# A second attention in four query tiles a head, with one shared tile for the last 16 queries of eight heads

## The reference, cut to what matters

```python
q = jnp.concatenate([q[..., :QK_NOPE_DIM], apply_rope(q[..., QK_NOPE_DIM:], cos, sin)], axis=-1)
k = jnp.concatenate([k_nope, jnp.broadcast_to(k_rope, (B, L, N_HEADS, QK_ROPE_DIM))], axis=-1)
for start in range(0, L, Q_BLOCK):
    s = jnp.einsum('bqhd,bkhd->bhqk', qb, kb).astype(jnp.float32) * scale
    s = jnp.where(mask[None, None], s, -jnp.inf)          # causal
    p = jax.nn.softmax(s, axis=-1).astype(vb.dtype)
    outs.append(jnp.einsum('bhqk,bkhd->bqhd', p, vb))
```

## Time and profile before

| | |
|---|---|
| median of 3 runs | 2306.0 us (2302.53 to 2307.81) |
| the profiled execution, its time and its span | 2310.08 us, 2308.3 us |
| granted TensorE clock, mean | 0.949 |
| PE busy, DVE busy, ACT busy, POOL busy | 89%, 42%, 43%, 38% |
| the second attention, first scores to the first product behind it | 1165.98 to 1337.28 us |

### The profile page before, as it was taken

The page is one execution under the profiler, slowest core; times in us unless marked ns, Lnnn a source line. Parts: engine busy times, 40 slices in busy tenths (PEclk is TensorE's granted clock), DMA queues, the critical chain, the costliest instruction groups (busy, mean ns, idle before and its releaser), DMA issues.

```text
span 2308.3 us, 35210 instructions
## 1 busy us (share of the span) xinstructions
PE 2043.1 (89%) x12788; PEld 1798.7 (78%) x12792; DVE 980.6 (42%) x1683; ACT 981.7 (43%) x1606; POOL 888.2 (38%) x498
## 2 busy tenths in 40 slices
PE   3699789998899999977878898999999669999997
PEld 2587577875677778756767787999999559999997
DVE  5862782115433422246667726242400674333202
ACT  2212663323555552243356625454522445555422
POOL 1244322432234344412643325434344554343443
PEclk8799998999999999987989999999999789999998
DMA  8372002321122233201200012323232003222232
GB/s 302 115 243 88 6 15 88 94 82 64 46 91 92 90 103 107 91 28 55 80 12 0 0 37 65 100 82 94 88 101 92 28 19 92 91 89 93 91 101 73
DMA packets 55370, 186.27 MB, mean 81 GB/s; under 512 B 6912, under 2 KB 10240, under 8 KB 55296
## 3 DMA queue, kind: packets, MB, share of 16 engines
q1 hardware_dynamic: 53920, 183.66, 24.6%
q10 hardware_dynamic: 1376, 1.59, 0.2%
HBM read 183.13 MB, written 2.10 MB: 80 GB/s over the span
## 4 chain that ended last, share of the span: by engine, by line
PE 76%; DVE 13%; issue 5%; ACT 3%; POOL 2%; DMA 1%; DVEq 0%; ACTq 0%; SPq 0%; POOLq 0%
PE PS L553 63%; PE PS L822 2%; PE PS L767 2%; PE PS L612 1%; PE PS L723 1%; PE PS L679 1%; DVE small L1967 1%; PE PS L600 1%; DVE ada_acc L1821 1%; DVE pool_s L298 1%; PE PS L740 1%; POOL X L1186 1%; DMA ada_w<-ada 1%; DVE small L1918 1%; DVE work L2080 1%
## 5 line engine op out<-in xcount | busy, mean ns | idle before, releaser
L1092 POOL TENSOR_TENSOR w_lo<-w_raw,w_hi 128x1024 fp32r<-128x1024 f32 x289 | 699.9, 2428 | 1131.8 <-ACT w_hi L1264 1130.6
L553 PE MATMUL PS<-H_hi,w_lo 128*128 128x264 f32 (+1 forms) x2152 | 584.7, 324 | 67.8 <-POOL H_lo L1226 25.8
L1264 ACT ACTIVATE w_hi<-w_raw 128x1024 fp32r<-128x1024 f32 x293 | 309.0, 1058 | 782.7 <-PE PS L553 717.2
L553 PE MATMUL PS<-H_lo,w_hi 128*128 128x264 f32 (+1 forms) x2152 | 576.0, 320 | 0.0
L553 PE MATMUL PS<-H_hi,w_hi 128*128 128x264 f32 (+1 forms) x2152 | 576.0, 320 | 0.0
L553 PEld LDWEIGHTS PS<-H_hi,w_lo 128*128 128x128 f32 x2152 | 365.7, 192 | 114.3 <-issue 45.1
L553 PEld LDWEIGHTS PS<-H_lo,w_hi 128*128 128x128 f32 x2152 | 367.5, 192 | 27.3
L553 PEld LDWEIGHTS PS<-H_hi,w_hi 128*128 128x128 f32 x2152 | 365.7, 192 | 28.1
L2080 DVE SCALAR_TENSOR_TENSOR work<-PS,vec,work 128x526 f32<-128x526 f32 (+3 forms) x264 | 188.3, 755 | 465.1 <-ACT work L1560 455.3
L553 PE MATMUL PS<-mid_hi,w_lo 128*128 128x264 f32 (+1 forms) x880 | 223.8, 308 | 3.6 <-DVE work L2080 3.6
L553 PE MATMUL PS<-mid_hi,w_hi 128*128 128x264 f32 (+1 forms) x880 | 223.1, 307 | 0.0
(11 more groups left out here) (257 smaller groups left out, 3048.1 us busy)
## 6 DMA issues: line engine op xcount, KB each, us to landing
w_raw<-stream SPq DMA_DIRECT2D x293, 512.0 KB, 3.5
ada_w<-ada SPq DMA_DIRECT2D x48, 512.0 KB, 5.9
X<-xT SPq DMA_DIRECT2D x1, 2048.0 KB, 9.6
yT<-X SPq DMA_DIRECT2D x8, 132.0 KB, 1.7
rel_raw<-rel ACTq DMA_DIRECT2D x4, 256.0 KB, 2.6
yT<-X SPq DMA_DIRECT2D x8, 124.0 KB, 1.7
vec<-vecs SPq DMA_DIRECT2D x1, 390.0 KB, 2.9
cos_t<-rope ACTq DMA_DIRECT2D x1, 264.0 KB, 2.8
```

Source lines behind the costliest of these rows:

```text
L553: last = pe.matmul(out[:, c0 + a:c0 + b], w, x[:, a:b], start=start and i == 0, stop=stop and i == 2)
L1092: gp.tensor_tensor(w_lo[:, o], w_raw[:, o], w_hi[:, o].bitcast(F32), ALU.subtract)\
L1264: return act_.activation(out, in_, ACT.Copy, scale=scale)
```

## The change

The second attention is written anew after the manner of the first one.

- **Units.** A head has four full tiles of 128 queries. The two heads of a pair take turns, tile by tile. The last 16 queries of eight heads (four pairs) stand below each other as one tile of 128 rows. With two such tails there are 66 units (`UNITS2`) instead of 80. A tail unit stands in the fourth and in the eighth pair, between the second and the third query tile.
- **Scores of the tail.** They build up over four pairs in a PSUM bank of their own (`tail_bank`). Each head puts its 16 queries at its own place in a window of zeros (`zq_hi`, `zq_lo`), so that a product of 128 rows adds only to its own 16. That is six products of 512 columns a pair (`tail_scores`). The scores of the 16 queries against the last 16 keys are six products of 16 columns and a mask, in a corner of the bank of the first tile of the odd head (`own_scores`). ACT copies them to `self_s`.
- **Ahead by two.** `scores` and `maximum` run two units ahead of `turn_over` and `normalize`. There are three score banks and four exponential buffers, and `weights` follows two units behind.
- **Staging.** Key parts hold the rotary rows too and are doubled over pairs. Query parts are rounded by tile (both heads, 256 columns). Values are split for all heads in the `uv` stage (ACT copies, DVE subtracts). The weights of the tail against all values are 60 products of 32 columns a group (`tail_outputs`).
- **Weight stream.** The transposed weights now lie over `w_raw`, so loads behind the first four `wo` blocks wait for the end of this attention.
- One small copy (`sel_tail`) is added to the set-up. The loops over pairs are unrolled.

The core of the diff, PE first:

```diff
+UNITS2 = []
+for _p in range(PAIRS2):
+    for _i in range(NQ1):
+        if _i == 2 and _p in TAIL_P2:
+            UNITS2.append((_p, None, None))
+        UNITS2 += [(_p, _i, 0), (_p, _i, 1)]
...
+                def scores(m):
+                    p, i, par = MAIN2[m]
+                    pe.wait_ge(kl2_ok, 2 * p + par + 1)
+                    pe.wait_ge(ql2_ok, NQ1 * p + i + 1)
...
+                    if m >= 3:
+                        pe.wait_ge(p2_ok, UNIT2[MAIN2[m - 3]] + 1)
...
+                    own = i == 0 and par == 1
+                    if own:
+                        own_scores(p, out)
...
+                def own_scores(p, out):
+                    pe.wait_ge(zl2_ok, p + 1)
+                    for par in range(2):
+                        tail_passes(out[:, own_bank2], p, par, slice(S1, S2), par == 0)
...
+                for u, (p, i, par) in enumerate(UNITS2):
+                    if i is not None and m < len(MAIN2):
...
+                        scores(m)
+                        if MAIN2[m][1:] == (1, 1):
+                            tail_scores(MAIN2[m][0])
+                        m += 1
...
+                    turn_over(u)
+                    if i == 2:
...
+                        outputs(p, par, False)
+                    elif i == 0 and p:
+                        outputs(p - 1, par, True)
+                    if i == 3 and par == 0 and p in TAIL_P2:
+                        tail_outputs(p // GROUP2)
```

POOL, ACT and DVE:

```diff
+                for p in range(1, PAIRS2):
+                    for par in range(2):
+                        lower_k(p, par)
+                    for i in range(NQ1 - 1):
+                        lower_q(p, i)
+                    lower_zq(p)
+                    lower_q(p, NQ1 - 1)
...
+                for u, (p, i, par) in enumerate(UNITS2):
+                    if u >= 2:
+                        weights(u - 2)
+                    exps(u)
+                    nxt = p + 1
+                    if i == 0 and par == 1 and p:
+                        round_q(p, 3)
+                    if nxt < PAIRS2:
+                        if i == 1:
+                            round_k(nxt, par)
+                        if i and par == 1:
+                            round_q(nxt, i - 1)
+                        if i == 3 and par == 1:
+                            round_zq(nxt)
+                    if i == 1 and p:
+                        take_out(p - 1, par)
...
+                for u, (p, i, par) in enumerate(UNITS2):
+                    if u >= 2:
+                        weights(u - 2)
+                    normalize(u)
+                    if u + 2 < len(UNITS2):
+                        maximum(u + 2)
+                    if i == 1 and p:
+                        take_out(p - 1, par)
...
-            for t in (k2_hi, k2_lo, v2_hi, v2_lo):
-                v.memset(t[:, :].bitcast(F32), 0.0).then_inc(zero_ok, 1)
```

More of the change, by code:

```diff
@@ L117 @@
 FOX1 = PAIRS1 // 2
+PAIRS2 = H2 // 2
+GROUP2 = 4
+TAIL_P2 = tuple(range(GROUP2 - 1, PAIRS2, GROUP2))
+UNITS2 = []
[4 more added lines that the diff above has]
+        UNITS2 += [(_p, _i, 0), (_p, _i, 1)]
+UNIT2 = {x: n for n, x in enumerate(UNITS2)}
+MAIN2 = [x for x in UNITS2 if x[1] is not None]
+ZQ = 112 + META + 112
 COL2 = 248
@@ L137 @@
 NVEC = _v
-SET_UP = 14
+SET_UP = 15
 ADA_ORDER = (1, 0, 2, 3, 4, 5)
@@ L704, in attention2 @@
             def attention2():
[L705 to L741, removed]
@@ L773, in step @@
[L773 to L777, removed]
-                    if t % nq == 3:
-                        outputs(p, t // nq, False)
-                    if t == nq + 1:
-                        outputs(p, 0, True)
-                    elif t == 1 and not first:
-                        outputs(p - 1, 1, True)
-                    turn_over(p, t)
@@ L791, in _ @@
+                for par in range(2):
+                    outputs(PAIRS2 - 1, par, True)
             pe.wait_ge(set_up, SET_UP)
@@ L1047, in _ @@
                 last.then_inc(w_used, 1)
-            for k in range(4):
-                pe.wait_ge(free[k], FREE0["wo"][k] + 1)
             attention2()
-            pe.wait_ge(o_lo, 8 + 1)
+            pe.wait_ge(o2_lo, 2 * PAIRS2)
+            pe.wait_ge(ot_lo, 2 * len(TAIL_P2))
             def ox2(k):
@@ L1545, in attention2, with round_q, round_zq @@
-                act_.wait_ge(pv_done, 2)
-                for i in range(ns):
-                    stage_head(0, 0, i)
-                over_pairs(act_, pairs, U, step)
-                weights(pairs - 1, U - 1)
-                take_out(pairs - 1)
+                def round_q(p, i):
+                    if p:
+                        act_.wait_ge(s2_full, 8 * (p - 1) + 2 * i + 2)
+                    copy(q_part2(q2_hi, i), q_raw2(p, i)).then_inc(qh2_ok, 1)
+                def round_zq(p):
+                    if p:
+                        act_.wait_ge(s2_full, 8 * (p - 1) + 5)
+                    copy(zq_part2(zq_hi), zq_raw2(p)).then_inc(zh2_ok, 1)
@@ L1552, in ffn @@
+                for u in range(len(UNITS2) - 2, len(UNITS2)):
+                    weights(u)
+                take_tail(1)
+                for par in range(2):
+                    take_out(PAIRS2 - 1, par)
             def ffn(up, down, T, layer, mid0):
@@ new lines, in normalize @@
+                def normalize(u):
+                    v.wait_ge(p2_ok, u + 1)
+                    c = u % 4
+                    s, q = small[:, 4 + c:5 + c], small[:, 8 + c:9 + c]
+                    if UNITS2[u][1] is None:
+                        chain.done(v.tensor_tensor(s, s, small[:, 12:13], ALU.add))
+                        chain.wait()
+                    chain.done(v.reciprocal(q, s))
+                    chain.wait()
+                    pb = p_buf2(u)
+                    v.tensor_scalar(pb, pb, q, None, ALU.mult).then_inc(pn2_ok, 1)
```

534 lines of the change are left out of this document (326 added, 208 removed).

## The result

The changed kernel takes 2321.4 us (median of five runs, 2320.7 to 2328.4) against 2306.0. The ratio is 1.0078, with a 95% interval of 1.006 to 1.0096. It is 15.4 us slower. The forecast was 2303 with a range of 2288 to 2317.

A forecast was written before the change was run, and what follows sets the result against it. No engine but the loop through PE, DVE and ACT was taken as the bound of the second attention. Its sum, 20.7 + 137.9 + 7.8 + 12.1 = 178.5 us against 181.4, gave 2306.0 - 2.9 = 2303, range 2288 to 2317.

The forecast's parts named there:

- from 0 to 1.45: In a pair, from PE turning over d of head 0 (time 0) until `lower_zq` lets the next a1 scores start.
- a0, b1, c0 and d0: Query tiles a to d of heads 0 and 1; PE was to idle 0.7, 1.3, 1.0, 0.5 us before their transposes.
- 18.7 to 18.8 and 0.3: A pair at full clock: PE's 13.9 us plus 4.9 idling; 0.3 added for DVE products that meet a POOL subtraction.
- The prices of the narrow products: PE products of few columns, in `own_scores` and the tail outputs, were taken at 0.115 us each.
- The rival of decoupled lists: Running ahead by two decouples the lists: a pair costs little over PE's sum, 15.3 us, kernel 2272; chance 0.08.
- the one of narrow products at double cost: Products with 16 rows or columns cost double: `own_scores` 0.5 us more a pair, tails 3 together; 2310; chance 0.07.
- I take 0.7, which is more than today's mean of 0.5: Clock falls were to cost 0.7 us a pair, out of 0 to 2, giving 19.7 us a pair.
- both places: At time 0 and at b1 in each new pair, PE works only about half of 3 us.
- 6.9 us of tail outputs on PE: A group's tail adds 60 products of 32 columns on PE, 6.9 us, counted behind each tail unit.
- the start: From the end of `uv` to d0 of the first pair turned over: 20.7 us, bounds 18 to 24.
- the end: Second group's tail outputs 6.9 us, last transposes and two late outputs 3.5, take-out to `wo` 1.7: together 12.1.
- The clock falls more often: Rival: falls at gaps around `own_scores` and b1 and in two blocks of 60 narrow products; 2315 (2311-2320); chance 0.22.

The follow-up runs named there:

- `zq` early: Changed kernel with `round_zq` moved one tile ahead on ACT and `lower_zq` two ahead on POOL: 2306.2 us.
- the wide block: Changed kernel with the tail outputs as 15 products of 512 columns a block instead of 60 of 32: 2312.1 us.
- The fill run: Changed kernel with dummy 256-column products where PE sits idle, before `own_scores` and the transposes of d0, a0, b1 and c0: 2319.6 us.
- the fixes: Three edits to the changed kernel: `round_zq` and `lower_zq` earlier (2306.2 us alone), tail scores behind c1's scores (2319.0), tail outputs as 512-column products (2312.1).
- all three: Changed kernel with `round_zq` and `lower_zq` earlier, tail scores behind c1's scores in six pairs, and 512-column tail outputs together: 2279.9 us.
- The fill run beside wide blocks: Changed kernel with dummy products in PE's gaps and tail outputs as 512-column products: 2302.4 us.
- the kernel with later tail scores: Changed kernel with `tail_scores` moved from behind b1's scores to behind c1's scores in six pairs: 2319.0 us.

## Why the prediction was wrong

**Right: the loop and its waits.** I forecast that PE would wait for `lower_zq` from 0 to 1.45. The trace has 1.31 us idle before `own_scores` in six of the seven later pairs; in the seventh the tail block hides it. The idle times of 0.7, 1.3, 1.0 and 0.5 us ahead of a0, b1, c0 and d0 are 0.57, 1.60, 0.96 and 0.46. At full clock the changed pair is 17.7 us (`zq` early, no fall) and 1.55 for the wait, or 19.2. My 18.7 to 18.8 and 0.3 make 19.1. The prices of the narrow products at full clock (0.115; measured 0.111) were right too. The rival of decoupled lists fell, and so did the one of narrow products at double cost as such.

**Wrong: the clock, in the pairs.** The step was "I take 0.7, which is more than today's mean of 0.5". The four plain pairs take 20.3, 23.4, 20.2 and 20.5 us from d0 to d0, a mean of 21.1. That is 1.9 above the 19.2, where the forecast has 0.7. Three of the pairs have one fall, which costs 1.0 to 1.3 us, and one has two, which cost 4.2. I had found both places where PE works half of the time, and then priced them by the old kernel, in which only every second pair falls.

**Wrong: the clock, in the narrow blocks.** The step was "6.9 us of tail outputs on PE". The blocks took 10.9 and 10.6, 7.7 us more in all, and left the clock low for what followed. The sum counted falls behind idling only, though the rival named these blocks. A stretch of narrow products with no idle time did the same, and the wide block without them did not.

**Wrong: the start and the end, in part.** The start took 22.9 us instead of 20.7. The first scores already come 6.0 us behind the end of `uv` instead of 4.8. The next fence shows why, from the timelines of POOL and DVE in the changed kernel: DVE's subtraction of 64x528 takes 0.70 us alone and 2.42 us beside POOL's subtraction for a weight block. The other 1.0 us of the start stays open. The end took 17.4 us instead of 12.1: 3.7 of it is the block. Most of the other 1.6 is the low clock behind the block: of the last 24 output products the first twelve take 2.6 us and the others 1.5.

```profile
1152.68 2.35 POOL L1187 TENSOR_TENSOR w_lo<-w_raw,w_hi 128x1024 fp32r<-128x1024 f32 x1 [6.32 <-ACT w_hi L1385]
1153.16 2.42 DVE L2120 TENSOR_TENSOR k_lo<-K,k_hi 64x528 fp32r<-64x528 f32 x1 [0.78 <-ACT k_hi L1385]
...
1156.81 0.70 DVE L2120 TENSOR_TENSOR k_lo<-K,k_hi 64x528 fp32r<-64x528 f32 x1
```

| from the end of `uv` | forecast | measured |
|---|---|---|
| to d0 of the first pair | 20.7 | 22.9 |
| the seven pairs and the first tail block | 145.7 | 156.9, of it 4.0 the block and 7.2 the pairs |
| to the start of `wo` | 12.1 | 17.4, of it 3.7 the block |
| sum | 178.5 | 197.1 |

One slip is of no weight: the forecast gives `uv` 0.7 us more (0.6 measured), but its sum, 20.7 + 137.9 + 7.8 + 12.1, leaves the 0.7 out.

**The rival that held.** "The clock falls more often" named both places and gave 2311 to 2320, with a chance of 0.22. It is what happened. It priced the pairs at 8 us (7.2 measured) and the blocks at 4 (7.7 measured). Start and end had no price in it, so its range ended 1 us too low. The Trainium skill (TensorE: Matmul & The Clock Gate, section "A second HAM failure mode: psum-queue depth-cycling") says that PE idling a little between groups, bank after bank, makes the clock go back and forth. The fill run agrees: with the gaps filled all four plain pairs stay at 1.00, and none of them did before. But I had let the trace of the old kernel outweigh the page, when it was the new kernel's gaps that counted.

**What the clock hides.** A fall costs about 1 us, and filling all gaps gave 1.8 us in 2321. From this one would say that the clock matters little. It mattered 9.7 us once the blocks were wide. At the same time the fixes gain more together (41.5 us) than singly (15.2 + 2.4 + 9.3 = 26.9); by the stages it is 40.4 against 28.7. The mean clock of the stage goes with this: 0.88, 0.81 and 0.87 with one fix, 0.95 with all three. That each fix takes away gaps or narrow stretches by which the others lost is my reading. The fill run beside wide blocks bears it out, and for the tail scores it isn't shown.

## What to carry to other kernels

A small operation behind a large one on two lists, here a 32-column rounding behind exponentials and a 256-column subtraction, can cost its wait once a round and the clock on top. Put it where its data are free, not where its turn comes. Don't price a stretch of PE by its columns alone. 60 products of 32 columns have a quarter of the columns of 15 products of 512, and were slower: 6.7 us at 0.111 us each, and 10.9 as the clock fell, against 3.9. When several stalls sit in one loop, try the fixes together before one of them is written off.

## What the runs showed of the hardware

- PE can lose its clock on narrow products though the profile shows it busy throughout. In the changed kernel 60 products of 32 columns, with PE idle for 0 us, ran 0.11 us apart for 3.3 us and then 0.21 apart to the end, at a granted clock of 0.50 (1.2 GHz). The same work as 15 products of 512 columns stayed at 1.00 (2.4 GHz) for its 3.9 us. It was so in 10 narrow blocks of 10 and in 8 wide ones of 8.
- The 16-column products in the pairs don't do that by themselves: with PE's gaps filled the clock was 1.00 in all four plain pairs.
- A DVE product of 128x256 that started with a subtraction of POOL took 1.48 us instead of the 0.35 of others of its shape, and ended 0.15 us behind it. Here is the pair of them in the kernel with later tail scores. The Trainium skill (SBUF — State Buffer, section "SBUF: two separate sides") says that one of the two holds their common port for a whole instruction and the other is blocked. The trace agrees with that.

```profile
1204.87 1.48 DVE L2160 TENSOR_SCALAR work<-work,small 128x256 f32<-128x256 f32 x1
```

```profile
1204.87 1.33 POOL L1255 TENSOR_TENSOR k_lo<-K,k_hi 64x528 fp32r<-64x528 f32 x1 [2.52 <-ACT k_hi L1385]
```
